# Sample keys joined behind the cached ones, values in plain fp32, and two reordered heads in a streaming encoder step

## The reference, cut to what matters

```python
# shared side: rows of the new frames, behind the cached ones for a sample
ckv_all   = concatenate([cache_ckv, ckv_new], axis=1)      # 512 + 16 rows for a sample
krope_all = concatenate([cache_krope, krope_new], axis=1)
k, v = expand_kv(ckv_all, krope_all, w_uk, w_uv)
s = einsum('bqhd,bshd->bhqs', q, k) * scale                # (prompt: chunk-causal mask)
o = einsum('bhqs,bshd->bqhd', softmax(s), v)
# linear attention, head by head, with the decay g of log_sigmoid gates
S_new = exp(b_last) * S + (k * exp(b_last - b)).T @ v
o = rmsnorm(o) * silu(gate)
```

## Time and profile before

| | us |
|---|---|
| median of 3 runs | 646.67 (646.52 to 646.95) |
| the profiled execution | 644.79 |
| its span | 643.0 |
| PE busy | 617.9 |
| PEld busy | 596.3 |
| DVE busy | 383.2 |
| ACT busy | 315.8 |
| POOL busy | 125.3 |

### The profile page before, as it was taken

How to read it: one execution, slowest core, us unless ns; L and a number is a source line. 1 busy time by engine, 2 the same in 40 slices (tenths; PEclk the granted TensorE clock), 3 DMA queues, 4 the chain that set the end, 5 groups by cost and what they waited for, 6 DMA issues and landing times.

```text
span 643.0 us, 12101 instructions
## 1 busy us (share of the span) xinstructions
PE 617.9 (96%) x4714; PEld 596.3 (93%) x4714; DVE 383.2 (60%) x574; ACT 315.8 (49%) x618; POOL 125.3 (19%) x140
## 2 busy tenths in 40 slices
PE   8998999999999879999999999999999999999996
PEld 7998999999999779999999999989999888899996
DVE  5475667355454674238664567557778877773415
ACT  6786464442462553236435433355555668872311
POOL 0110010010030152216425410211000118650001
PEclk9999999999999989999999999999999999999998
DMA  8923262270262262234234420321001046766004
GB/s 301 345 82 92 90 199 73 87 215 28 74 197 67 74 229 66 86 87 173 67 93 112 127 66 2 114 70 47 34 18 50 13 151 209 252 196 229 2 1 165
DMA packets 66281, 73.69 MB, mean 115 GB/s; under 512 B 8112, under 2 KB 58544, under 8 KB 66096
## 3 DMA queue, kind: packets, MB, share of 16 engines
q1 hardware_dynamic: 66224, 72.91, 35.8%
HBM read 62.12 MB, written 10.78 MB: 113 GB/s over the span
## 4 chain that ended last, share of the span: by engine, by line
PE 65%; DVE 15%; ACT 10%; issue 4%; DMA 3%; POOL 2%; SPq 1%; DVEq 0%; ACTq 0%; POOLq 0%
PE bank L1563 21%; PE bank L1564 20%; PE bank L1565 20%; DVE slab_lo L1260 2%; DMA x_nat<-in_x_sample_dram 2%; ACT prob L1194 2%; DVE pT_lo L1260 2%; ACT slab_hi L991 1%; PE bank L1610 1%; DVE sT_lo L1260 1%; ACT sT_hi L991 1%; ACT qS L991 1%; DVE stat L1540 1%; DMA x_raw<-in_xT_dram 1%; DVE rows L1256 1%
## 5 line engine op out<-in xcount | busy, mean ns | idle before, releaser
L1563 PE MATMUL bank<-slab_hi,hat_hi 128*128 128x256 f32 (+2 forms) x600 | 171.0, 285 | 3.8 <-DVE rows L1423 1.8
L1564 PE MATMUL bank<-slab_lo,hat_hi 128*128 128x256 f32 (+2 forms) x600 | 169.8, 283 | 0.0
L1565 PE MATMUL bank<-slab_hi,hat_lo 128*128 128x256 f32 (+2 forms) x600 | 169.8, 283 | 0.0
L1563 PEld LDWEIGHTS bank<-slab_hi,hat_hi 128*128 128x128 f32 x600 | 115.2, 192 | 5.0 <-DVE rows L1423 2.0
L1564 PEld LDWEIGHTS bank<-slab_lo,hat_hi 128*128 128x128 f32 x600 | 115.2, 192 | 0.0
L1565 PEld LDWEIGHTS bank<-slab_hi,hat_lo 128*128 128x128 f32 x600 | 115.2, 192 | 0.0
L1260 DVE TENSOR_TENSOR slab_lo<-stage,slab_hi 128x1024 fp32r<-128x1024 f32 (+3 forms) x70 | 84.8, 1212 | 24.9 <-ACT slab_hi L991 23.4
L1563 PE MATMUL bank<-hat_hi,slab_hi 128*128 128x320 f32 x256 | 79.8, 312 | 0.9 <-DVE rows L1487 0.8
L1565 PE MATMUL bank<-hat_hi,slab_lo 128*128 128x320 f32 x256 | 79.1, 309 | 0.0
L1564 PE MATMUL bank<-hat_lo,slab_hi 128*128 128x320 f32 x256 | 79.1, 309 | 0.0
L991 ACT ACTIVATE slab_hi<-stage 128x1024 fp32r<-128x1024 f32 (+3 forms) x70 | 71.0, 1014 | 10.2 <-issue 3.6
(11 more groups left out here) (340 smaller groups left out, 1434.2 us busy)
## 6 DMA issues: line engine op xcount, KB each, us to landing
stage<-in_a_w_in_dram SPq DMA_DIRECT2D x22, 512.0 KB, 5.2
stage<-in_b_w_in_dram SPq DMA_DIRECT2D x10, 512.0 KB, 3.8
st_s<-in_state_gla_dram SPq DMA_DIRECT2D x4, 1024.0 KB, 6.7
out_dram<-st_s SPq DMA_DIRECT2D x4, 1024.0 KB, 4.9
stage<-in_a_w_out_dram SPq DMA_DIRECT2D x8, 512.0 KB, 4.3
stage<-in_ckvT_dram SPq DMA_DIRECT2D x8, 512.0 KB, 4.1
stage<-in_cache_ckv_dram SPq DMA_DIRECT2D x8, 512.0 KB, 4.0
stage<-in_b_w_out_dram SPq DMA_DIRECT2D x8, 512.0 KB, 3.5
```

Source lines behind the costliest of these rows:

```text
L1563: pe.matmul(out, a[0], b[0], start=first, stop=False)
L1564: pe.matmul(out, a[0], b[1], start=False, stop=False)
L1565: return pe.matmul(out, a[1], b[0], start=False, stop=last)
```

## The change

The code is in four parts.

1. `steps()`, first head: lgh(2) and lgh(3) move up beside ln(1) and lg(1), lgh(1) between g0(3) and g0(4), qlo(0) ahead of the weight piece, and kT(0) ahead of c(2) and c(3).
2. `steps()`, last head: the order os, Us, o, gl(2) becomes Us, o, os, gl(2). The step Us loses ACT's scaling of the states, which is a step Ux of its own, in the last head behind gl(2). As Us may now stand ahead of os, DVE's part waits until PE has read the old states in os. On POOL, the pieces of ("wo","A",1) wait for gl(3) on DVE and those of ("gb",3) for lcn.
3. Samples: the 16 new keys of a stream are copied by POOL (step ot, four small copies) behind its 512 cached ones. ss multiplies 528 columns in two halves of 264, one at the end of one bank and one at the start of the next. The products with `ones` and `others` go, and their constants. ACT makes two exponentials, of 512 and of 16 columns; the remaining columns of the fifth probability tile are set to zero by POOL (step zr). PE waits for ot before ss.
4. Samples' values: sv takes probabilities and cached rows in plain fp32, the rows straight from the stage buffer, in 5 products. spT_lo, cn_hi, cn_lo and cn_s_lo go, and with them ACT's and POOL's part of cs. The buffer is free when PE has ended sv. The ring has 8 buffers in this stage, two of them where qN and kN were.

```diff
-NWIDE = 6
+NWIDE = 8
+KEYS = PAST + SL
+FIRST_KEY = PAST - KEYS // 2
@@ steps, first head
-    out += [..., ("ln", 3), ("lg", 3), ("ln", 1), ("lg", 1)]
-    out += [("g0", 3), ("g0", 4), ("c", 0), ("em",), ("e", 0), ("lgh", 1), ("piece", ("qk", 1), 0), ("q", 0), ("lgh", 2), ("lgh", 3), ("qlo", 0), ("k", 0), ("klo", 0)]
-    out += [("c", 1), ("c", 2), ("kT", 0), ("c", 3)]
+    out += [..., ("ln", 3), ("lg", 3), ("ln", 1), ("lgh", 2), ("lg", 1), ("lgh", 3)]
+    out += [("g0", 3), ("lgh", 1), ("g0", 4), ("c", 0), ("em",), ("e", 0), ("q", 0), ("qlo", 0), ("piece", ("qk", 1), 0), ("k", 0), ("klo", 0)]
+    out += [("c", 1), ("kT", 0), ("c", 2), ("c", 3)]
@@ steps, end of a head
-        out += [("os", h), ("Us", h, 0), ("Us", h, 1), ("sts", h)]
         if last:
-            out += [("o", h), ("ldr",)]
-            out += [("gl", t) for t in range(EARLY_GATE, NT - 1)] + [("oT", 0), ("gl", NT - 1)]
+            out += [("Us", h, 0), ("Us", h, 1), ("o", h), ("os", h), ("gl", EARLY_GATE), ("Ux", h, 0), ("Ux", h, 1), ("sts", h), ("ldr",)]
+            out += [("gl", t) for t in range(EARLY_GATE + 1, NT - 1)] + [("oT", 0), ("gl", NT - 1)]
         else:
+            out += [("os", h), ("Us", h, 0), ("Us", h, 1), ("Ux", h, 0), ("Ux", h, 1), ("sts", h)]
@@ samples
-        out += [("st", b)]
+        out += [("st", b)] + [("zr", b + 2)] * (b + 2 < SB)
         if b + 3 < SB:
-            out += [("ct", b + 3), ("cr", b + 3)]
-        if b + 1 < SB:
-            out += [("cs", b + 1)]
+            out += [("ct", b + 3), ("cr", b + 3), ("ot", b + 3)]
...
-        out += [("sv", b)]
+        out += [("sv", b), ("cs", b)]
@@ POOL
+                    if name == ("wo", "A", 1):
+                        after(pool, "dve", "gl", EARLY_GATE + 1)
+                    if name == ("gb", 3):
+                        after(pool, "dve", "lcn")
+                elif kind == "ot":
+                    for to, x in ((sT_hi, cT_s[0]), (sT_lo, cT_s[1])):
+                        pool.tensor_copy(to[b % 2][:, :, PAST:KEYS], x[:, :, mine])
+                    pool.tensor_copy(skS[b % 2][:, PAST:KEYS], krS[:, mine])
+                    last = pool.tensor_copy(skL[b % 2][:, PAST:KEYS], krL[:, mine])
@@ ACT, ss
+                    after(act, "pool", "zr", b)
+                    act.activation(sprob[b % 2][:, 0:NT - 1, :], row[:, FIRST_KEY:FIRST_KEY + PAST]..., ACT.Exp, ...)
+                    last = act.activation(sprob[b % 2][:, NT - 1, b * SL:(b + 1) * SL], row[:, FIRST_KEY + PAST:FIRST_KEY + KEYS], ACT.Exp, ...)
@@ PE, ss and sv
+                    for half in range(2):
+                        c0 = half * (KEYS // 2)
+                        keys = slice(c0, c0 + KEYS // 2)
+                        o = row[:, FIRST_KEY + c0:FIRST_KEY + c0 + KEYS // 2]
                         for c in range(KC):
+                            mm3(o, cut(qab, A_, c, b), cut((sT_hi[b % 2], sT_lo[b % 2]), A_, c, keys), c == 0, False)
+                        pe.matmul(o, q, skS[b % 2][:, keys], start=False, stop=False)
+                        last = pe.matmul(o, q, skL[b % 2][:, keys], start=False, stop=True)
...
+                        x = staged_as("cs", ("cs", b))[:, s, :] if s < NT - 1 else cn_s[:, :]
+                        last = pe.matmul(bank[:, 0, 0:KL], spT[:, s * P:(s + 1) * P], x, start=s == 0, stop=s == NT - 1)
```

More of the change, by code:

```diff
@@ L46 @@
 CONST, NCONST = columns((("ident", P), ("mask_p", P), ("mask_s", P), ("parity", 2), ("cos", NT * RH), ("sin", NT * RH)))
-CONST_R, NCONST_R = columns((("cum_p", P + 2), ("cum_s", P + 2), ("early", P), ("late", P), ("ones", P), ("others", 2 * P)))
+CONST_R, NCONST_R = columns((("cum_p", P + 2), ("cum_s", P + 2), ("early", P), ("late", P)))
 def slabs():
@@ L610, in program @@
         sprob = [sb("sprob0", [P, NT, P])]
-        for i in range(NSTAGE, NWIDE):
-            place[0] = qlT_at + 4 * D * (i - NSTAGE + 2)
-            stage.append(sb(f"stage{i}", [P, PIECE]))
+        for i in range(2):
+            place[0] = qlT_at + 4 * D * (i + 2)
+            stage.append(sb(f"stage{NSTAGE + i}", [P, PIECE]))
         place[0] = qS_at
@@ L630, in program @@
         place[0] = temp_at
-        spT = pair("spT", [P, TOK])
+        spT = sb("spT", [P, TOK])
         place[0] = prob_at
@@ L647, in put @@
             return sb(name, shape, dt)
[L649 to L655, removed]
+        wide = 4 * KC * KEYS
+        sT_hi = [put(block_at[(4, 0)[i]], f"sT_hi{i}", [P, KC, KEYS], fp32r) for i in range(2)]
+        sT_lo = [put(block_at[4] + (wide, 3 * wide)[i], f"sT_lo{i}", [P, KC, KEYS], fp32r) for i in range(2)]
+        skS = [put((block_at[4] + 2 * wide, block_at[0] + wide)[i], f"skS{i}", [P, KEYS], fp32r) for i in range(2)]
+        skL = [put((block_at[4] + 2 * wide + wide // 2, qlT_at + 1024)[i], f"skL{i}", [P, KEYS], fp32r) for i in range(2)]
+        assert block_at[4] + 4 * wide <= phase_at and block_at[0] + wide + wide // 2 <= block_at[2] and 1024 + wide // 2 <= 4 * D
+        for i, at in enumerate((qN_at, kN_at)):
+            stage.append(put(at, f"stage{NSTAGE + 2 + i}", [P, PIECE]))
         place[0] = lat_gain_at
@@ L779, in load_stage @@
                     after(sp, "pe", "vh", 1, NP - 1)
+                    if STAGE_OF[n] >= NSTAGE + 2:
+                        after(sp, "pe", "S", HB - 1, 1)
+                        after(sp, "pe", "qabs", HB - 1)
+                elif STAGE_OLD[n] is not None and STAGED[STAGE_OLD[n]][0] == "cs":
+                    after(sp, "pe", "sv", STAGED[STAGE_OLD[n]][1])
                 elif STAGE_OLD[n] is not None:
@@ L963, in _ @@
                     last = pool.tensor_scalar(r, r, 1.0 / D, EPS, MUL, ADD)
-                elif kind == "cs":
-                    after(pool, "act", *step)
-                    b = step[1] % 2
-                    last = pool.tensor_tensor(cn_lo[b][:, :, :], staged_as(kind, step), raw(cn_hi[b][:, :, :]), SUB)
                 elif kind == "cr":
@@ L1154, in _ @@
                     after(act, "dve", "lcn")
-                    last = copy(cn_s[0][:, :], ckvn[:, NP, :])
+                    last = copy(cn_s[:, :], ckvn[:, NP, :])
                 elif kind == "cT":
@@ L1203, in _ @@
                     else:
-                        after(act, "pe", "O", (1, 4)[b])
-                    last = copy(sT_hi[b % 2][:, :, :], staged_as(kind, step))
+                        after(act, "pe", "O", 4 + b)
+                    last = copy(sT_hi[b % 2][:, :, 0:PAST], staged_as(kind, step))
                 elif kind == "cr":
@@ L1516, in _ @@
                     b = step[1]
-                    last = low(sT_lo[b % 2][:, :, :], staged_as("ct", step), sT_hi[b % 2][:, :, :])
+                    last = low(sT_lo[b % 2][:, :, 0:PAST], staged_as("ct", step), sT_hi[b % 2][:, :, 0:PAST])
                 elif kind == "S":
@@ L1876, in constants @@
     row = (i == 0).astype(np.float32)[:, None]
-    others = np.full(2 * P, NEG, np.float32)
-    others[P:P + SL] = 0.0
     const = [np.eye(P), before, before * same, (i[:, None] // SL % 2 == np.arange(2)[None, :]), np.cos(ang), np.sin(ang)]
-    const_r = [cum_p, cum_s, row * (1 - half.T * 0 - (i >= P // 2)[None, :]), row * np.where(i >= P // 2, NEG, 0.0)[None, :], row * np.ones((1, P)), row * others[None, :]]
+    const_r = [cum_p, cum_s, row * (1 - half.T * 0 - (i >= P // 2)[None, :]), row * np.where(i >= P // 2, NEG, 0.0)[None, :]]
     return [np.ascontiguousarray(np.concatenate(x, axis=1).astype(np.float32)) for x in (const, const_r)]
```

103 lines of the change are left out of this document (51 added, 52 removed), and 4 rows, old and new, of the table PARTS.

## The result

The changed kernel takes 625.91 us (median of 4 runs, 625.43 to 626.32) where the kernel before takes 646.60; the ratio is 0.9681, with a 95% interval of 0.9667 to 0.9695. That is 20.7 us less. The forecast was 636.8 us, 9.9 us less, with a range of 633.0 to 640.0: the sign was right, the size wrong by 10.9 us.

What follows compares the result with a forecast made beforehand. The prediction took TensorE, busy for 617.9 of 643.0 us, to bound the kernel. Its terms 2.7 + 6.6 + 0.6 = 9.9 us, off 646.67, gave 636.8 us, range 633.0 to 640.0.

Steps and rivals of the forecast that it cites:

- The smaller const_r and the tail change nothing: Closing remark on the samples: fewer constants and the changed tail were given no effect on the time.
- Part 1: First head: five steps moved, so TensorE's stalls on lg_hi, kt and kn_lo go; 2.7 us gained.
- rival C: First head: reordering delays k(0) by the table load before g0(3)'s tanh, half the gain lost; 638.1 us, chance 0.11.
- Part 2: Last head: new order lets oT(0) start 6.2 us earlier and y(A,0) 6.6 us earlier; 6.6 us gained.
- The stall before o: Last head: o must wait for Slo, which DVE ends at 214.03; a new stall of 1.0 us.
- Rival B: Last head: POOL's steps for o stretch under DVE's state sum, oT(0) 1 to 2 us later; 638.3 us, chance 0.18.
- gl(4)'s product: Last head: DVE's product meets POOL's at 228.9, ends about 230.7; y starts at 232.0, not 231.3.
- Part 3: Samples: ACT, DVE and POOL's gate, not TensorE, set most of the pace; 0.6 us gained by the end of sv(7).
- Rival A: Samples run at TensorE's own pace, gaining 5.9 us in place of 0.6; 631.5 us, chance 0.12.
- rival D: Samples: POOL's four ot copies cost 1.83 us each, 7.3 us a sample; slower, 648.8 us, chance 0.03.

Runs made afterwards that it cites:

- after_shift64: The changed kernel with 64 bytes of SBUF left empty behind const_r; 634.91 us.
- first_head_only: The kernel before with only the first head's new order, tiles at their old places; 642.57 us, ratio 0.9934.
- last_head_only: The kernel before with only the last head's new order, Ux and the two waits on POOL; 642.22 us, ratio 0.9926.
- samples_only: The changed kernel with both heads in the old order and hat and all behind it at their old places; 647.05 us, ratio 0.9987.
- before_shift32: The kernel before with 32 bytes left empty behind const_r; 646.87 us in one execution.
- before_shift64: The kernel before with 64 bytes left empty behind const_r; 641.40 us, ratio 0.9911.
- before_hatlo64: The kernel before with 64 bytes left empty between hat_hi and hat_lo; 645.31 us in one execution.

## Why the prediction was right or wrong

**The step that failed** is one the sum did not have: "The smaller const_r and the tail change nothing." The removal of 384 columns of constants moved every tile behind them by an odd multiple of 64 bytes, and some 2000 products became faster: 8.0 us of the trace's 19.1, in the three stretches where nothing was edited, and about 0.6 more inside the last head. after_shift64, the change with most of this taken back, took 634.91 us, in the forecast range. Its spacing is 0.1187, not the 0.1199 of the kernel before; over 2000 products that is 2.4 us, so at unchanged spacing it would have taken some 637 us, an estimate that lies at the forecast of 636.8. None of the rivals, nor the bounds, had it. Why the places change the spacing stays open.

**Part 1**, 2.7: 2.9 in the trace and 2.8 in first_head_only. DVE's kt and the records behind it, to be set beside the earlier trace rows:

```profile
47.60 0.42 DVE L1336 SCALAR_TENSOR_TENSOR rows<-rows,bank 128x256 f32<-128x256 f32 x1 [0.31 <-ACT rows L1071]
...
55.49 0.82 DVE L1277 TENSOR_TENSOR kt<-bank,Em 128x640 f32<-128x640 f32 x1 [0.58 <-PE bank L1585]
```

kt came at 55.49 (forecast 55.95). The bank of g0(3) was free at 48.02, not 48.6, and k(0) started at 48.12, so rival C did not come about. Not foreseen: all five other traces that keep these stalls show the lower clock behind them, so the part is probably worth more on such chips (4.3 us in first_head_only).

**Part 2**, 6.6: 7.3 in the trace with the new places, 6.1 in last_head_only. The order of events is the one forecast, on PE, DVE and POOL, to be set beside the earlier trace rows:

```profile
211.15 1.07 PE L1723 MATMUL bank<-st_s,q_own 128*32 128x256 f32 x16
218.07 1.04 PE L1630 MATMUL bank<-const,rows 128*128 128x128 f32 x8
...
225.22 0.39 PE L1583 MATMUL bank<-slab_hi,hat_hi 128*128 128x256 f32 x1
```

```profile
213.25 2.48 DVE L1277 TENSOR_TENSOR st_s<-bank,st_s 128x1024 f32<-128x1024 f32 x2 [1.27 <-PE bank L1585]
...
222.96 0.42 DVE L1277 TENSOR_TENSOR rows<-rows,st_in 128x256 f32<-128x256 f32 x1
```

```profile
213.62 1.04 POOL L957 TENSOR_TENSOR stat<-stat,minus_half 128x4 f32<-128x4 f32 x1
...
221.19 7.90 POOL L934 TENSOR_TENSOR stage<-stage,gain_a_head_norm 128x1024 f32<-128x1024 f32 x4 [4.73 <-DVE rows L1277]
```

The first transpose came 6.9 us behind os and ran at once and at full clock (eight in 1.04 us, not 1.94). The stall before o was 1.4, not 1.0. Rival B did not come about. One of POOL's four steps took 1.04 us, but it takes that without DVE as well, as in the kernel before, where DVE was idle from 222.1 to 228.15:

```profile
226.72 1.04 POOL L947 TENSOR_TENSOR stat<-stat,minus_half 128x4 f32<-128x4 f32 x1
```

So nothing stretched; the prediction had taken the price of an addition (0.20) for this power. The chain ended 3.1 us behind ACT's last square and not 1.4, and had that to spare. gl(4)'s product was to end 1.8 us after its start because of POOL and delay y by 0.7. It took 0.42, as it began at 222.96, 0.12 us before the end of POOL's first product, so neither of the two prices was put to the test. This error and the stall cancel in part.

**Part 3**, 0.6: 0.45 in the trace with the new places, 0.12 in samples_only. Its terms, on PE, ACT and POOL, answer to the earlier trace rows:

```profile
516.96 0.36 PE L1583 MATMUL bank<-sT_hi,qab_hi 128*128 128x264 f32 x1 [0.56 <-POOL sprob L999]
...
519.00 1.89 PE L1856 MATMUL bank<-stage,spT 128*128 128x256 f32 x8
520.72 0.59 PE L1856 MATMUL bank<-cn_s,spT 128*128 128x256 f32 x2
521.15 0.71 PE L1847 MATMUL bank<-const,sprob 128*128 128x128 f32 x5
```

```profile
526.38 0.69 ACT L1248 ACTIVATE sprob<-bank,stat 128x512 f32<-128x512 f32 x1 [1.49 <-DVE stat L1561]
...
533.10 0.69 ACT L1248 ACTIVATE sprob<-bank,stat 128x512 f32<-128x512 f32 x1 [1.69 <-DVE stat L1561]
...
538.53 0.69 ACT L1248 ACTIVATE sprob<-bank,stat 128x512 f32<-128x512 f32 x1 [1.49 <-DVE stat L1561]
```

```profile
521.73 0.21 POOL L987 CAST sT_hi<-cT_s_hi 128x32 fp32r<-128x32 f32 x1
521.88 0.21 POOL L987 CAST sT_lo<-cT_s_lo 128x32 fp32r<-128x32 f32 x1
522.03 0.20 POOL L989 CAST skS<-krS 128x16 fp32r<-128x16 f32 x1
```

Scores 2.04 us (forecast 2.0), values 2.15 (2.15), copies 0.15 apart (0.15), exponentials 6.72 and 5.43 us apart (6.6 and 5.4). Rival A (TensorE's own pace) and rival D (copies at 1.83 each) did not happen. Of the waits forecast for POOL before ss(3) to ss(7), only those of ss(3) and ss(7) were there (0.76 and 1.61 us); ss(5) and ss(6) waited for ACT's exponential (1.44 and 0.32). What the forecast did not see is that two rounds run side by side, so that shortening the one it named would have gained nothing.

## What to carry to other kernels

When an edit changes the size of any tile, compare the placement of all others too, and count the records of a stretch that the edit does not touch: a shift of 64 bytes was worth more here than either reordering. Test a gain by its parts and by a kernel that has only the side effect; two near-equal rounds need both edits at once, and each alone can be slower.

## What the hardware showed

- At full clock, products of 256 columns in fp32r with slab0 or slab1 were 0.120 us apart in the kernel before, with the stationary tile 32 bytes further 0.117, 64 bytes further 0.113 or 0.118, 128 bytes further 0.119, 192 bytes further 0.118. Products of 320 columns, with the roles of the tiles exchanged, took 0.147 in all of these. Which of its two values place 64 gives is not fixed by the program, and not explained.
- The first head's stalls (three, 2.3 us in all) stood ahead of a clock of 0.50 from 62 to 66 us in five traces on two chips (before_shift32, before_shift64, before_hatlo64, samples_only, last_head_only), which cost 2.2 us in last_head_only and 3.3 in before_shift64. first_head_only, without the stalls and on one of these chips, was granted 1.00. The profile of the kernel before has the stalls and 1.00 there (mean 0.994); most of its other executions have means of 0.984 to 0.990, and where in them the clock fell is not on record.
- A GpSimd power of 128 partitions by 4 columns took 1.04 us, with DVE idle and with DVE summing states; a product of the same shape took 0.20.
